# The last gate panel pair of an input projection: from block products to plain units between attention steps, and a reordering of finishes at an FFN seam

## The reference

```python
proj = h @ w_in[l]                       # 1024 x 1024 times 1024 x 5120
bg, cg, u, q, k, v, ga, gb = jnp.split(proj, split_pts, axis=-1)
y_conv = short_conv_branch(bg, cg, u, conv_w[l]) @ w_proj_conv[l]
o = stick_breaking_attention(q, k, v)    # 8 heads of 64; A = sigmoid(z) * prod (1 - sigmoid(z)), s < t
y_attn = o @ w_proj_attn[l]
merged = jax.nn.sigmoid(ga) * y_conv + jax.nn.sigmoid(gb) * y_attn
mix_out = merged @ w_out[l]
```

## Time and profile before

| what | us |
|---|---|
| median of 3 runs | 2784.45 |
| lowest and highest | 2779.55 and 2785.67 |
| the profiled execution | 2784.28 |
| its span | 2782.5 |
| block products of the input projection, first to last matmul | 1442.6 to 1788.8 |
| attention steps with their fills | 1788.9 to 1986.6 |

### The profile page before, as it was taken

One profiled execution on the slowest core, in us unless ns is written; L12 is line 12 of the kernel. 1 busy time (PEld: TensorE's weight loads), 2 busy tenths in 40 slices (PEclk: granted clock), 3 DMA queues, 4 the chain that ended last, 5 costly groups with the idle time before them and its releaser, 6 DMA issues.

```text
span 2782.5 us, 39285 instructions
## 1 busy us (share of the span) xinstructions
PE 2646.0 (95%) x15530; PEld 2138.3 (77%) x15530; DVE 1879.6 (68%) x2265; ACT 1236.9 (44%) x2316; POOL 405.8 (15%) x354
## 2 busy tenths in 40 slices
PE   7999998999799999999899999999998999999997
PEld 6887556888688888888778888656677888888886
DVE  3466554664687777888974664489746755578889
ACT  3323565332777773333553333467316433333332
POOL 4322001347300000000200000001275000000002
PEclk9999999999999999999999999999999999999999
DMA  3210000004356664332322222421252333343323
GB/s 135 61 31 16 7 6 24 3 19 174 105 167 212 189 197 163 117 121 106 136 91 106 76 91 102 160 72 35 84 200 105 108 105 108 121 161 112 121 106 121
DMA packets 213488, 290.49 MB, mean 104 GB/s; under 512 B 16551, under 2 KB 143806, under 8 KB 213310
## 3 DMA queue, kind: packets, MB, share of 16 engines
q1 hardware_dynamic: 195918, 227.75, 24.9%
q10 hardware_dynamic: 17392, 60.30, 5.5%
HBM read 220.91 MB, written 67.11 MB: 104 GB/s over the span
## 4 chain that ended last, share of the span: by engine, by line
PE 77%; DVE 11%; ACT 4%; POOL 3%; issue 3%; DMA 2%; SPq 0%; ACTq 0%; DVEq 0%; POOLq 0%
PE ps L1739 7%; PE ps L1740 7%; PE ps L1741 7%; PE ps L1794 6%; PE ps L1796 5%; PE ps L1795 5%; PE ps L1877 4%; PE ps L1878 4%; PE ps L1879 4%; PE ps L1530 3%; PE ps L1436 2%; PE ps L1309 1%; PE ps L1310 1%; PE ps L1311 1%; PE ps L1458 1%
## 5 line engine op out<-in xcount | busy, mean ns | idle before, releaser
L1794 PE MATMUL ps<-down_t_hi,down_s_hi 128*128 128x512 f32 x896 | 349.5, 390 | 3.9 <-DVE acc L3332 2.2
L1796 PE MATMUL ps<-down_t_hi,down_s_lo 128*128 128x512 f32 x896 | 348.7, 389 | 0.0
L1795 PE MATMUL ps<-down_t_lo,down_s_hi 128*128 128x512 f32 x896 | 348.7, 389 | 0.0
L2492 ACT CAST down_s_hi<-down_a 128x2048 fp32r<-128x2048 f32 x56 | 107.2, 1915 | 368.7 <-PE ps L1796 327.1
L1142 POOL TENSOR_SCALAR mean_sq<-ssq 128x1 f32<-128x1 f32 x64 | 36.2, 565 | 1301.7 <-ACT squares_junk_ffn L2030 1250.4
L1739 PE MATMUL ps<-act_hi,up_hi 128*128 128x512 f32 (+1 forms) x544 | 205.7, 378 | 6.1 <-issue 2.8
L1740 PE MATMUL ps<-act_lo,up_hi 128*128 128x512 f32 (+1 forms) x544 | 204.9, 377 | 0.0
L1741 PE MATMUL ps<-act_hi,up_lo 128*128 128x512 f32 (+1 forms) x544 | 204.8, 377 | 0.0
L1794 PEld LDWEIGHTS ps<-down_t_hi,down_s_hi 128*128 128x128 f32 x896 | 168.2, 188 | 41.7 <-issue 7.4
L1796 PEld LDWEIGHTS ps<-down_t_hi,down_s_lo 128*128 128x128 f32 x896 | 168.2, 188 | 35.3
L1795 PEld LDWEIGHTS ps<-down_t_lo,down_s_hi 128*128 128x128 f32 x896 | 168.2, 188 | 34.6
(11 more groups left out here) (383 smaller groups left out, 6513.5 us busy)
## 6 DMA issues: line engine op xcount, KB each, us to landing
down_a<-hid_spill SPq DMA_DIRECT2D x32, 1024.0 KB, 6.6
hid_spill<-up_hid ACTq DMA_DIRECT2D x30, 1024.0 KB, 6.3
w_ada<-in_w_ada SPq DMA_DIRECT2D x48, 512.0 KB, 3.9
up_raw<-in_w_in SPq DMA_DIRECT2D x18, 1024.0 KB, 5.1
raw<-in_w_out SPq DMA_DIRECT2D x32, 512.0 KB, 3.8
up_raw<-in_w_up SPq DMA_DIRECT2D x16, 1024.0 KB, 5.5
down_b<-in_w_down SPq DMA_DIRECT2D x16, 1024.0 KB, 6.5
up_raw<-in_w_mlp_in SPq DMA_DIRECT2D x16, 1024.0 KB, 5.4
```

The source lines that it names most:

```text
L1794: pe.matmul(out, ops["s_hi"][:, k, cols], ops["t_hi"][:, k, :], start=first, stop=False, skip_group_check=True)
L1795: pe.matmul(out, ops["s_hi"][:, k, cols], ops["t_lo"][:, k, :], start=False, stop=False, skip_group_check=True)
L1796: mm = pe.matmul(out, ops["s_lo"][:, k, cols], ops["t_hi"][:, k, :], start=False, stop=last, skip_group_check=True)
```

## The change

**The gate pair.** `IN_STEPS` is 17: the eighth gate step, columns 768 to 1023 of `gb`, is no longer a block step. Its 256 columns are loaded as before and split as a whole (`gate_hi` by ACT, `gate_lo` by DVE, 128x2048 each), and 32 plain units of three matmuls (`gate_unit`, 96 matmuls of 128x512) compute them: 8 behind the last block product, the others in fours behind the steps 0, 1, 3, 5, 7 and 8. The upper token columns of four of the eight feature blocks hold a difference by then (the operand of block product 5), so that result is the sum of a part in PSUM and a part that ACT copied out (`gate_part`), added by DVE. ACT's `gate_take` does the two copies, the sigmoids and the store.

**What else moves.** The first scores are issued ahead of the last block product. The splits of `y` move from steps 5 to 8 to steps 10 to 13 (`Y_FIRST`). The 56 fills begin at step 15 instead of 10, at 11 units in 10 steps: two units behind steps 24, 34, 44, 54 and 64. Transposed weights have two homes (`sb_at_homes`), since the activations stay in place until the gate units are done; loads of q, k and v of pairs 1 to 3 are ordered anew on SP. Banks of even and odd block steps change places (`in_bank`), so the first step waits for other copies of `v`.

**The seam.** For the first FFN, `ffn_finish` of tiles 1, 2 and 3 comes before `down_x(run, 1, 0)` and the takes of the last product.

```diff
-IN_STEPS = len(IN_COLUMNS)
+IN_STEPS = len(IN_COLUMNS) - 1
...
-FILL_FIRST = 10
+GATE_UNITS = (0, 1, 2, 3, 8, 9, 10, 11, 12, 13, 14, 15, 4, 5, 6, 7, 16, 17, 18, 19, 20, 21, 22, 23, 24, 25, 26, 27, 28, 29, 30, 31)
+GATE_STEPS = (8, 4, 4, 0, 4, 0, 4, 0, 4, 4)
+SB_AT_EARLY = 12
+Y_FIRST = 10
+FILL_FIRST = 15
...
-    return min(max(step - FILL_FIRST, 0), FILL_IN_STEPS)
+    return min(max((step - FILL_FIRST) * 11 // 10, 0), FILL_IN_STEPS)
...
-            return 3 * (u % 2) + UP_BANK[p]
+            return 5 - 3 * (u % 2) + UP_BANK[p]
...
-                        pe.wait_ge(sem("v2_done"), {1: 5, 2: 6, 5: 7}[p])
+                        pe.wait_ge(sem("v2_done"), {1: 2, 2: 3, 5: 4}[p])
...
-            for n in range(IN_TOTAL):
-                in_product(n)
+            def gate_unit(m):
+
+                j, q, k = m // 16, m // 8 % 2, m % 8
+                b = 6 if (j, q) == (0, 1) else 5
+                if m == 0:
+                    pe.wait_ge(sem("in_lo"), FROM["in_lo"] + IN_TOTAL + 1)
+                    pe.wait_ge(sem("in_copied"), FROM["in_copied"] + IN_COPY_AT[IN_STEPS - 1, 4])
+                elif m == 8:
+                    pe.wait_ge(sem("in_out"), FROM["in_out"] + IN_OUT_AT[IN_STEPS - 1, 2])
+                elif m in (4, 16, 20, 24):
+                    gate_copied(pe, {4: 1, 16: 2, 20: 3, 24: 4}[m])
+                out, w = ps[:, b, :].rearrange("p (h c) -> p h c", h=2), slice(j * P, (j + 1) * P)
+                hi, lo = (by_block(x[:, k, :], q) for x in acts)
+                pe.matmul(out, gate_hi[:, k, w], hi, start=(k == 0), stop=False, skip_group_check=True)
+                pe.matmul(out, gate_hi[:, k, w], lo, start=False, stop=False, skip_group_check=True)
+                mm = pe.matmul(out, gate_lo[:, k, w], hi, start=False, stop=(k == KD - 1), skip_group_check=True)
+                if m in (3, 7, 15, 19, 23, 31):
+                    mm.then_inc(sem("in_prod"), 1)
...
+                if step + 1 < len(GATE_STEPS):
+                    gate_units(step)
                 for m in range(fill_first_unit(step), fill_first_unit(step + 1)):
                     fill_unit(m)
 
-            sb_scores(0, 0, 0)
+            for n in range(IN_TOTAL):
+                if n == IN_TOTAL - 1:
+                    sb_scores(0, 0, 0)
+                in_product(n)
+            gate_units(-1)
...
+            def gate_take(step):
+
+                if step == 1:
+                    in_store(IN_STEPS - 1)
+                if step in (1, 4):
+                    gate_made(act, step)
+                    act.copy(gate_part[:], ps[:, 5, :]).then_inc(sem("in_copied"), 1)
+                elif step in (2, 6):
+                    gate_made(act, 3 if step == 2 else 5)
+                    act.activation(gate_cols(step // 6, 0), ps[:, 5, :].rearrange("p (h c) -> p h c", h=2), ACT.Sigmoid)\
+                        .then_inc(sem("in_copied"), 1)
+                elif step == 3:
+                    gate_summed(act, 1)
+                    act.activation(gate_cols(0, 1), gate_cols(0, 1), ACT.Sigmoid)
+                elif step == Y_FIRST:
...
-                down_x(run, 1, 0)
-                ffn_finish(run, tag, row, 1)
                 if run == 0:
-                    R5.split_low(dve, 1)
+                    for t in (1, 2, 3):
+                        ffn_finish(run, tag, row, t)
+                        if t == 1:
+                            R5.split_low(dve, 1)
+                    down_x(run, 1, 0)
+                else:
+                    down_x(run, 1, 0)
+                    ffn_finish(run, tag, row, 1)
...
+                elif step in (1, 9):
+                    gate_made(dve, 2 if step == 1 else 6)
+                    gate_copied(dve, 1 if step == 1 else 3)
+                    bank, part = (x.rearrange("p (h c) -> p h c", h=2) for x in (ps[:, 6 if step == 1 else 5, :], gate_part[:]))
+                    dve.tensor_tensor(gate_cols(step // 9, 1), bank, part, ALU.add).then_inc(sem("in_out"), 1)
```

More of the change, by code:

```diff
@@ L178 @@
 IN_COLUMNS += [base + 2 * P * n for base in (IN2_GA, IN2_GB) for n in range(4)]
-IN_STEPS = len(IN_COLUMNS)
+IN_STEPS = len(IN_COLUMNS) - 1
 IN_CONV, IN_GATES = 4, 10
-IN_KEPT = [u for u in range(IN_STEPS) if not IN_CONV <= u < IN_GATES]
+IN_KEPT = [u for u in range(IN_STEPS + 1) if not IN_CONV <= u < IN_GATES]
 def in_order():
@@ L1073, in _ @@
             in_load(1)
-            for u in range(2, IN_STEPS):
+            for u in range(2, IN_STEPS + 1):
                 sp.wait_ge(sem("in_lo"), FROM["in_lo"] + IN_AT[u - 2, 4] + 1)
@@ L1880, in in_product, with gate_units @@
                 mm.then_inc(sem("in_prod"), 1)
-            for n in range(IN_TOTAL):
-                in_product(n)
+            def gate_unit(m):
[15 more added lines that the diff above has]
+                    mm.then_inc(sem("in_prod"), 1)
+            def gate_units(step):
+                first = sum(GATE_STEPS[:step + 1])
+                for m in GATE_UNITS[first:first + GATE_STEPS[step + 1]]:
+                    gate_unit(m)
             def fill_unit(m):
@@ L2650, in sb_weights_out @@
             def sb_weights_out(i, s):
-                for n, g in enumerate(sb_turns(s)):
-                    w = sb_width(i, s, n)
+                for f, g in enumerate(sb_turns(s)):
+                    w = sb_width(i, s, f)
                     act.wait_ge(sem("sb_turned"), SB_GROUPS * i + g + 1)
-                    if SB_GROUPS * i + g >= SB_AT_SLOTS:
-                        act.wait_ge(sem("sb_pv"), sb_turn_position(SB_GROUPS * i + g - SB_AT_SLOTS) + 1)
-                    act.copy(sb_at[g % SB_AT_SLOTS][:, 0:w], ps[:, SB_TURN_BANKS[g % 2], 0:w]).then_inc(sem("sb_at_done"), 1)
+                    n = SB_GROUPS * i + g
+                    if n >= SB_AT_SLOTS and not SB_AT_EARLY <= n < SB_AT_EARLY + SB_AT_SLOTS:
+                        act.wait_ge(sem("sb_pv"), sb_turn_position(n - SB_AT_SLOTS) + 1)
+                    act.copy(sb_at(i, g)[:, 0:w], ps[:, SB_TURN_BANKS[g % 2], 0:w]).then_inc(sem("sb_at_done"), 1)
             def sb_out(i, half):
```

114 lines of the change are left out of this document (82 added, 32 removed).

## The result

The changed kernel takes 2794.15 us (median of six runs) against 2784.36 us beside it: 1.0038 times as long, interval 1.0027 to 1.0048, about 10 us slower. One of the six runs took 4036.45 us at a mean clock of 0.67 and is left out of the comparison; without it the median is 2794.03. The profiled execution took 2794.32 us, span 2792.5. I had forecast 2780.5, faster than before, and a range up to 2788.0: it came out slower, and above the range.

The account below looks back on a forecast made before the run. PE was taken as the bound, with DVE also nearly full in the later attention; -19.0 + 12.3 + 3.6 + 2.5 - 3.2 = -3.8 gave 2780.5 us, range 2771.5 to 2788.

Parts of the forecast that it names:

- seam: First FFN's seam: tile 3's finish starts earlier, PE's idle falls from 9.45 to 6.3 us, kept to the end: minus 3.2.
- block step gone: Block products: 84 matmuls of 0.2267 us leave PE, where nothing covered them: minus 19.0 us.
- from there to the scan of item 10: Steps 0 to 9: gate units fill PE and it waits 3.9 us on ACT; item 10's scan 9.7 us later.
- to the scan of item 15: Steps 10 to 14: the split of `y` on ACT and DVE, partly offset by fills that leave: plus 2.6 us.
- doubled units: Second fill units behind steps 24, 34, 44 at 0.89 each, those behind 54 and 64 0.9 together: plus 3.6 us.
- waits for merges: From step 15: PE's fills wait for DVE merges at six new panel ends, 1.1 us at step 22; 2.5 taken.
- Rival 1: Steps 0 to 14 and fills: gate units hide, merges find DVE free, sum -12.6, 2771.7 us; chance 0.32.
- the bound of 6.6: From step 15: what six places of late merges would cost in full; zero was held possible too.
- Rival 2: Steps 10 to 14: PE's clock falls and stays low about 24 us into step 15: +12, 2792 us; chance 0.10.

Follow-up runs that it names:

- e6_no_gate_work: e1_in_phase with 90 of the gate units' 96 matmuls left out, 6 kept as signals, all waits, copies and sums kept; 2766.71 us.
- e2_merge_first: Changed kernel with DVE's merge ahead of the mask where a panel ends behind steps 18, 22, 54, 58, 62; 2786.05 us, ratio 1.0008.
- e9_pool_late: e1_in_phase with one more POOL wait, holding the proj weights' splits for panels 2 to 6 four steps longer; 2782.77 us, ratio 0.9992.
- e1_in_phase: Changed kernel with one fill unit behind each of steps 15 to 65, two behind 17, panels ending at their old items; 2786.7 us, ratio 1.0005.

## Why the prediction was wrong, step by step

| term | predicted | in the profile after |
|---|---|---|
| ahead of the seam | 0 | +1.7 |
| seam | -3.2 | -3.5 |
| block step gone | -19.0 | -18.8 (1440.9 to 1769.4, less 1.1 of early scores, against 1442.6 to 1788.8) |
| from there to the scan of item 10 | +9.7 | +10.6 |
| to the scan of item 15 | +2.6 | +3.3 |
| from there to that of item 63: doubled units | +3.6 | } |
| and waits for merges | +2.5 | } +15.2 |
| behind it | 0 | +1.5 |
| sum | -3.8 | +10.0 |

- **What held.** The block products' term, the seam and the first ten steps are right to about 1 us. PE waited for ACT in steps 3, 5 and 7 for 1.72, 0.24 and 1.72, where I had 1.6, 0.6 and 1.7; the clock was 1.00 through step 9. Rival 1, that the gate units hide, is out: e6_no_gate_work shows that they cost 16 to 20 of their 20.4 us, so that nearly only the start's idle pays for the block step.
- **What failed** is the term for waits for merges. I named six places (22, 44, 47, 54, 58, 62); all six are there. I had put a price of 1.1 on each, and then took 2.5 for all, because "DVE's merges leave other places free". They free nothing: before the change no fill waits in the steps. They measured 8.1 in the six places and 10.1 in eight; steps 18 and 33 I had not named. Even the bound of 6.6 was too low, and so the range was. With 10.1 in the place of 2.5 the sum is +3.8, 2788.1: this term alone turns faster into slower. The other 6.2 of the miss are 1.7 ahead of the seam, 1.6 in steps 0 to 14, 1.5 behind them, 1.5 behind the scan of item 63, less 0.1 for seam and block step together.
- **Why it was mis-sized.** The price of a place was right in kind: the six measured 1.36 in the mean, and at 47, 54, 58 and 62 it is, by e2_merge_first and the rows, mostly the wide tile that I had looked at. The discount had no row behind it. What I had overlooked is the order across engines: mask behind the next step's scores, merge behind the mask, fill behind the merge. This needs no wide tile, so step 18 costs 1.15 just as well, and the fills one step later cost at all 13 places. I had the order of DVE and of PE for it; I did not lay the two beside each other for one such step.
- **What was missing** is the clock. Doubled units cost 4 x 0.89 = 3.6 by estimate, and 15.2 - 10.1 - 3.6 = 1.5 seems to be all that is left, but waits for merges take the place of other waits in part. The busy times give the better account. From the scan of item 15 to the next stage, after:

```profile
1830.90:1995.70 164.80, 146.98 (x1030) 97.12 (x1030) 130.07 (x141) 98.83 (x236) 21.50 (x14) 0.96 0.15 46
```

Beside the 149.0 us of the earlier trace rows that is 15.8 more. PE is idle 6.7 more (17.8 and 11.1) and busy 9.1 more. Five units more lie in the stretch, 5 x 0.68 = 3.4; the other 5.7, by this estimate, are the same work at a lower clock (turning eight blocks took 1.91 us at 1932.95, where it takes 1.09 at full clock). The sum had no term for that behind step 14. DVE's overlap with POOL's splits falls in that stretch too; e9_pool_late shows that the place of the splits is worth 3 to 4 us by itself (pairs and medians). I had not thought of POOL at all: the fills move its work too.

- **Rival 2** ended on the right side for the wrong reason. It had the clock fall in steps 10 to 14 and stay low. It fell there (0.82), was still low from 1830 to 1834 (0.63), came back, and cost little; the falls that cost more came later, behind the waits of steps 47, 54 and 58, and what made the kernel slower was the step I had put at 2.5. (PE's busy time in the gap that this rival starts from is 0.36 of 2 us; 0.30 is that of the weight loads. Nothing hangs on it.)
- **Ahead of the seam** nothing was changed. The later 1.6 is there at 34 us of the span already (DVE's row at 33.69 before, 35.31 after). In eleven kernels with the seam's new order and the same code ahead of it, these turns start anywhere from 1377.7 to 1382.2. So a single profile says nothing on 2 us between kernels; the comparisons above start at the first scan, and times are medians.

## What to carry to other kernels

Work that is woven into a steady loop has a phase, and its price depends on the phase more than on its amount: one step later cost 20 us with nothing added. When such work is moved, write out for one place what each engine has in front of the handover and behind it, on both engines, and price it at every place; a wait that shows up in the working is not to be set off against room elsewhere. It can cost the clock behind it as well, 4.3 us in one pair here. Move also everything that follows it, down to the engine that seems idle: here POOL's weight splits.

## What was not expected of the hardware

- DVE and POOL slow each other when both run on two inputs in SBUF: 128x1024 scan 3.36 instead of 2.28 us, 128x512 subtraction on POOL 2.12 instead of 1.29. The profile shows it as duration, not as a wait, so no view of waits has it.
- The granted clock falls after the same wait in one run and not in another. PE waited 1.72 in step 7 in each of e1_in_phase, e9_pool_late and the changed kernel. In e9_pool_late the next stretch was at 0.62, in the two others at 1.00; the four gate units behind it began 4.5 us ahead of the work that follows them, where they took 2.9 in the changed kernel. Below first e9_pool_late, then the changed kernel. What tells them apart was not found; it is a second reason why traces of single runs differ by 1 or 2 us.

```profile
1792.00:1796.00 4.00, 2.28 (x16) 1.56 (x13) 1.15 (x3) 2.92 (x8) 0.00 (x0) 0.95 0.00 0
1796.00:1800.00 4.00, 4.00 (x15) 2.85 (x14) 3.51 (x4) 0.62 (x2) 0.00 (x0) 0.62 0.00 0
```

```profile
1796.00:1800.00 4.00, 2.28 (x29) 1.74 (x28) 1.86 (x2) 2.04 (x5) 0.00 (x0) 1.00 0.00 0
1800.00:1804.00 4.00, 4.00 (x24) 2.90 (x26) 3.22 (x4) 1.50 (x5) 0.00 (x0) 1.00 0.00 0
```
